# x in two token halves around the first modulation unit, context ahead of the last weights, index query and small projection at 356 columns

## The reference

```python
mod_x = (silu_c @ w_ada[i] + b_ada[i])[:, None, :]
sh1, sc1, g1, sh2, sc2, g2 = jnp.split(mod_x, N_MOD, axis=-1)
hx = modulate(rms_norm(x, norm1_g[i]), sh1, sc1)      # first block
hc = modulate(rms_norm(ctx, norm1_g[i]), csh1, csc1)  # ctx: 256 tokens
qx, kx, vx, ux = split_proj(hx @ w_in[i])
kvc = hc @ w_in[i][:, ATT_DIM:3 * ATT_DIM]
...
h = rmsnorm(x, norm_mix[layer])                       # second block
proj = h @ w_in[layer]
qa, ka, va, qb, kb, vb, qi, ki, wi, ga, gb = jnp.split(proj, IN_OFFSETS, axis=-1)
qi = rope(qi.reshape(B, T, IDX_HEADS, IDX_DIM), pos)
ki = rope(ki[:, :, None], pos)[:, :, 0]
```

## Time and profile before

| | us |
|---|---|
| median of 3 runs (729.28 to 729.64) | 729.4 |
| the profiled execution | 729.7 |
| its span | 727.9 |
| PE busy | 715.3 (98%) |
| PEld busy | 574.6 (79%) |
| DVE busy | 517.4 (71%) |
| ACT busy | 411.2 (56%) |
| POOL busy | 24.6 (3%) |

### The profile page before, as it was taken

One profiled execution on the slowest core, in us unless ns is written; L12 is line 12 of the kernel. 1 busy time (PEld: TensorE's weight loads), 2 busy tenths in 40 slices (PEclk: granted clock), 3 DMA queues, 4 the chain that ended last, 5 costly groups with the idle time before them and its releaser, 6 DMA issues.

```text
span 727.9 us, 9700 instructions
## 1 busy us (share of the span) xinstructions
PE 715.3 (98%) x3766; PEld 574.6 (79%) x3766; DVE 517.4 (71%) x911; ACT 411.2 (56%) x691; POOL 24.6 (3%) x43
## 2 busy tenths in 40 slices
PE   7999999999999999999999999999999999999996
PEld 6668885578888888888888777778888888888885
DVE  4689999898666866847898799765857455545544
ACT  4477658986754563556546676675455444344432
POOL 1030012001000000000110000000000000000000
PEclk9999999999999999999999999999999999999999
DMA  9995939617556576643548333453376566555511
GB/s 367 413 378 184 389 105 359 222 59 259 194 186 233 206 280 222 242 174 115 161 167 301 140 117 121 159 178 121 116 231 231 174 185 204 189 174 174 174 58 59
DMA packets 72990, 145.94 MB, mean 201 GB/s; under 512 B 4129, under 2 KB 27681, under 8 KB 71921
## 3 DMA queue, kind: packets, MB, share of 16 engines
q1 hardware_dynamic: 71136, 140.03, 55.0%
q0 software_dynamic: 1520, 5.03, 1.9%
q10 hardware_dynamic: 288, 0.27, 0.1%
HBM read 144.27 MB, written 1.05 MB: 200 GB/s over the span
## 4 chain that ended last, share of the span: by engine, by line
PE 87%; DVE 5%; ACT 2%; DMA 2%; issue 2%; SPq 0%; POOL 0%; POOLq 0%; DVEq 0%
PE bank L441 22%; PE bank L443 22%; PE bank L442 22%; PE bank L785 5%; PE bank L423 5%; PE bank L783 3%; DMA WX<-in_w_ada 2%; DVE WL L1573 2%; PE bank L460 1%; PE bank L917 1%; PE bank L939 1%; PE bank L623 1%; PE bank L782 1%; PE bank L514 1%; PE bank L481 1%
## 5 line engine op out<-in xcount | busy, mean ns | idle before, releaser
L1573 DVE TENSOR_TENSOR WL<-W,WH 128x1024 fp32r<-128x1024 f32 (+2 forms) x222 | 249.6, 1170 | 36.2 <-ACT WH L1070 36.1
L1070 ACT ACTIVATE WH<-W 128x1024 fp32r<-128x1024 f32 (+2 forms) x222 | 211.8, 1011 | 52.2 <-DMA W<-in_w_mlp 36.3
L441 PE MATMUL bank<-WH,AHL 128*128 128x512 f32 (+1 forms) x480 | 189.1, 394 | 0.8 <-DVE WL L1573 0.4
L443 PE MATMUL bank<-WH,AHL 128*128 128x512 f32 (+1 forms) x480 | 185.4, 386 | 0.0
L442 PE MATMUL bank<-WL,AHL 128*128 128x512 f32 (+1 forms) x480 | 185.2, 386 | 0.0
L441 PEld LDWEIGHTS bank<-WH,AHL 128*128 128x128 f32 x480 | 90.2, 188 | 22.8 <-issue 4.0
L443 PEld LDWEIGHTS bank<-WH,AHL 128*128 128x128 f32 x480 | 90.1, 188 | 18.6
L442 PEld LDWEIGHTS bank<-WL,AHL 128*128 128x128 f32 x480 | 90.3, 188 | 16.9
L441 PE MATMUL bank<-WH,HH 128*128 128x512 f32 (+1 forms) x218 | 84.9, 390 | 0.0
L443 PE MATMUL bank<-WH,HL 128*128 128x512 f32 (+1 forms) x218 | 84.5, 388 | 0.0
L442 PE MATMUL bank<-WL,HH 128*128 128x512 f32 (+1 forms) x218 | 84.4, 387 | 0.0
(11 more groups left out here) (287 smaller groups left out, 852.8 us busy)
## 6 DMA issues: line engine op xcount, KB each, us to landing
W<-in_w_mlp SPq DMA_DIRECT2D x32, 1024.0 KB, 5.4
W<-in_w_in SPq DMA_DIRECT2D x24, 1024.0 KB, 5.7
W<-in_w_gate SPq DMA_DIRECT2D x22, 512.0 KB, 4.2
W<-in_w_up SPq DMA_DIRECT2D x22, 512.0 KB, 5.2
W<-in_w_down SPq DMA_DIRECT2D x11, 1024.0 KB, 5.0
W<-in_w_ada SPq DMA_DIRECT2D x10, 1024.0 KB, 8.5
WX<-in_w_ada SPq DMA_DIRECT2D x10, 1024.0 KB, 10.4
W<-in_w_out SPq DMA_DIRECT2D x8, 1024.0 KB, 5.7
```

Of the source, the lines that this page charges most:

```text
L441: e.matmul(po, hs, wh[:, k, c0:c0 + cw], start=first and k == 0, stop=False)
L443: ins = e.matmul(po, ls, wh[:, k, c0:c0 + cw], start=False, stop=last and k == unit.nk - 1)
L1070: e.activation(m.WH[unit.slot][:, c], m.W32[unit.slot][:, c], ACT.Copy).then_inc(S["w_hi"], 1)
L1573: e.tensor_tensor(m.WL[unit.slot][:, c], m.W32[unit.slot][:, c], m.WH[unit.slot][:, c].bitcast(F32), ALU.subtract).then_inc(S["w_lo"], 1)
```

## The change

- **x by tokens.** `XT` and `xsq` are laid out as two halves of 128 tokens with all eight k. SP issues x half 0, modulation unit 0, x half 1, then the rest. ACT squares each half in two operations; the adds of DVE (`xpair`, `xfour`) are gone, and PE sums each half with eight matmuls of one column. Statistic, power and spread are done for each half by itself, and `modulate_x`, `high_x`, `low_x` of k = 0 too. On PE the order is now `mod_first(0)`, spread 0, turn 0, sums 1, `ab(0, 0)`, spread 1, `mod_first(1)`, turn 1, `ab(0, 1)`; from e8 = 1 on as before. Fewer idle matmuls (`keep_busy`).
- **Context.** `XC` is loaded ahead of the last `ab` unit. ACT: first square of the context, high part of the last `ab` unit, `high_x(7)`, high part of a `k` unit, second square, high part of the next. DVE: first statistic inside the step k = 7, first scaling, low part, second statistic, second scaling, low part.
- **356 columns.** The units `qi` hold the first 356 columns of the index query, the units `s` its last 156 columns with the 200 small ones. The list's order is qi, qi, s, s, qb, qb, and PE's order in `first2` qi, s, qb, with tile 1's transposes between the two halves of tile 0's `qb`. ACT copies one bank more for each tile. In ACT's second `between` the unit is split in two halves, one behind the second square of the first half of X and one behind the first square of the second half, not in one piece; the `hi(2)` behind it stays. The order of DVE's rope calls and ACT's copies follows the new counts.

```diff
@@ Mem
-        self.XT = M("XT", 0, [128, 8, 256])
-        self.xsq = M("xsq", 24, [128, 8, 256])
+        self.XT = M("XT", 0, [128, 2, 8, 128])
+        self.xsq = M("xsq", 40, [128, 2, 8, 128])
@@ weight_units
-    two("qi", "w_in_2", 2176, True, "qi_mm", (3, 4))
+    two("qi", "w_in_2", 2176, True, "qi_mm", (3, 4), 356)
+    for i in range(2):
+        add("s", "w_in_2", 4 * i, 4, [("w_in_2", 2532, 156), ("w_in_2", 2048, 128), ("w_in_2", 2688, 72)], True, ("s_mm", 3 + i))
     two("qb", "w_in_2", 1536, True, "p2_mm", (3, 4))
-    for i in range(2):
-        add("s", "w_in_2", 4 * i, 4, [("w_in_2", 2048, 128), ("w_in_2", 2688, 72)], True, ("s_mm", 3 + i))
@@ sync_program
-    for h in range(2):
-        e.dma_start(m.XT[:, 4 * h:4 * h + 4, :], d["xt"][h].rearrange("p (k t) -> p k t", k=4)).then_inc(S[f"l_x{h}"], 16)
-    for n in range(16):
+    x_half(0)
+    load(0)
+    x_half(1)
+    for n in range(1, 15):
         load(n)
     e.dma_start(m.XC[:, :, :], d["ctx"].rearrange("(t p) n -> p t n", p=128)).then_inc(S["l_xc"], 16)
-    for n in range(16, len(units)):
+    for n in range(15, len(units)):
@@ tensor_program
+    def x_sums(tb):
+
+        for k in range(8):
+            w.wait_ge(S["sq_sum" if k > 3 else "x_sq"], tb + 1)
+            ins = e.matmul(bank[5 + tb][:, 0:1], m.xsq[:, tb, k, :], m.ones[:, 0:1], start=k == 0, stop=k == 7)
+        ins.then_inc(S["sums"], 1)
+        frees(5 + tb, ("mean_sq", tb + 1))
...
+    keep_busy(7)
     x_sums(0)
+    keep_busy(2)
+    mod_first(0)
+    x_spread(0)
+    mod_turn(0, 4)
     x_sums(1)
+    ab(0, 0)
+    x_spread(1)
+    frees(7, ("setup", 5))
+    mod_first(1)
+    mod_turn(1, 6)
+    ab(0, 1)
+    for e8 in range(1, 8):
@@ first2
-        product(by["qi"], m.AH, m.AL, tb, 4 + tb, "qi_mm", n_ready(1, tb))
-        product(by["qb"], m.AH, m.AL, tb, tb, "p2_mm", n_ready(1, tb))
-        if tb == 0:
-            norm_turn(3, 1)
-        product(by["s"], m.AH, m.AL, tb, 2 + tb, "s_mm", n_ready(1, tb), 200)
+        product(by["qi"], m.AH, m.AL, tb, 4 + tb, "qi_mm", n_ready(1, tb), 356)
+        product(by["s"], m.AH, m.AL, tb, 2 + tb, "s_mm", n_ready(1, tb), 356)
+        product(by["qb"], m.AH, m.AL, tb, tb, "p2_mm", n_ready(1, tb), 512, None if tb else lambda: norm_turn(3, 1))
@@ scalar_program
-    hi()
     w.wait_ge(S["l_xc"], 16)
     square(2, m.XC[:, 0, :], m.XC2[:, 0, :])
+    hi()
     high_x(7)
+    hi()
     square(3, m.XC[:, 1, :], m.XC2[:, 1, :])
-    hi(2)
+    hi()
...
-    def between(tb, mid):
+    def between(tb):
         i = 8 + 4 * tb
+        halves = high_halves(tb)
         for n in range(2):
             for j in range(2):
                 w.wait_ge(S["btw"], 8 * tb + 3 * n + 2 + j)
                 square(i + 2 * n + j, m.X[:, tb, 512 * n:512 * n + 512], m.S1[:, tb, 512 * n:512 * n + 512])
-            hi(mid[n])
+                if n != j:
+                    next(halves, None)
...
     w.wait_ge(S["m2_mm"], 64)
     hi(2)
@@ vector_program
-            rows_out(k)
+    for k in range(1, 8):
+        rows_out(k)
         modulation(k)
         modulate_x(k)
+        if k == 7:
+            mean_square(2, (2,))
         lo()
         low_x(k)
-    mean_square(2, (2,))
+    hat(m.XC, m.XC2, 0, 2, "c_hat")
+    lo()
     mean_square(3, (3,))
-    lo()
-    hat(m.XC, m.XC2, 0, 2, "c_hat")
     hat(m.XC, m.XC2, 1, 3, "c_hat")
     lo()
```

More of the change, by code:

```diff
@@ L510, in ab @@
         ls = m.AL[:, e8, tb * 128:tb * 128 + 128]
-        w.wait_ge(S["mx_act"], e8 + 1)
+        w.wait_ge(S["mx_act"], e8 + 2 if e8 else tb + 1)
         for n in range(2):
@@ L521, in ab, with x_spread @@
                      stop=e8 == 7).then_inc(S["b_mm" if n else "a_mm"], 1)
[L523 to L533, removed]
-        w.wait_ge(S["l_id"], 16)
[L535 to L542, removed]
+    def x_sums(tb):
[4 more added lines that the diff above has]
+        frees(5 + tb, ("mean_sq", tb + 1))
+    def x_spread(tb):
+        w.wait_ge(S["l_id"], 16)
+        w.wait_ge(S["rstd"], tb + 1)
+        e.matmul(bank[7][:, tb * 128:tb * 128 + 128], m.stat[:, 40 + tb:41 + tb].to_broadcast([128, 128]), m.ident[:, :],
+                 start=True, stop=True).then_inc(S["sums"], 1)
+    keep_busy(7)
     x_sums(0)
-    keep_busy(3)
+    keep_busy(2)
+    mod_first(0)
+    x_spread(0)
+    mod_turn(0, 4)
     x_sums(1)
[L546 to L550, removed]
+    ab(0, 0)
[5 more added lines that the diff above has]
+    for e8 in range(1, 8):
         if e8 < 7:
@@ L887, in tensor_program @@
         product(by["ka"], m.AH, m.AL, tb, tb, "p2_mm", n_ready(1, tb))
[L888 removed]
+        frees(tb, ("p2_out", tb + 11))
         dots(4 * tb)
@@ L1086, in from_bank, with high_x @@
         copy(o, bank[b][:, cols], done, scale)
-    def high_x(k):
-        w.wait_ge(S["mx_dve"], k + 1)
-        e.activation(m.AH[:, k, :], m.hT[:, k, :], ACT.Identity, bias=m.mod1[:, k, 0, 0:1]).then_inc(S["mx_act"], 1)
+    def high_x(k, ts=slice(0, 256)):
+        w.wait_ge(S["mx_dve"], k + 2 if k else ts.stop // 128)
+        e.activation(m.AH[:, k, ts], m.hT[:, k, ts], ACT.Identity, bias=m.mod1[:, k, 0, 0:1]).then_inc(S["mx_act"], 1)
     def modulate_c(i, n):
@@ L1105, in two, with x_square @@
         return hT[:, 2 * i:2 * i + 2, :].rearrange("p a b -> p (a b)")
-    def half_of(t, h):
-        return t[:, 4 * h:4 * h + 4, :].rearrange("p a b -> p (a b)")
+    def x_square(tb):
+        w.wait_ge(S[f"l_x{tb}"], 16)
+        for h in range(2):
+            ks = slice(4 * h, 4 * h + 4)
+            e.activation(m.xsq[:, tb, ks, :], m.XT[:, tb, ks, :], ACT.Square,
+                         scale=1.0 / 32).then_inc(S["sq_sum" if h else "x_sq"], 1)
     e.dma_start(m.cs[:, :], d["cs"]).then_inc(S["l_cs"], 16)
@@ L1112, in scalar_program @@
     e.activation(m.cs[:, :], m.cs[:, :], ACT.Silu).then_inc(S["silu_c"], 1)
[L1113 to L1116, removed]
+    x_square(0)
+    x_square(1)
+    first = high_halves(1)
+    next(first)
+    high_x(0, slice(0, 128))
+    next(first)
+    next(first, None)
+    high_x(0, slice(128, 256))
+    for k in range(1, 7):
         hi()
         high_x(k)
-        if k == 1:
+        if k == 2:
             e.activation(m.stat[:, 92:93], m.stat[:, 94:95], ACT.Sigmoid)
-    hi()
     w.wait_ge(S["l_xc"], 16)
     square(2, m.XC[:, 0, :], m.XC2[:, 0, :])
+    hi()
     high_x(7)
+    hi()
     square(3, m.XC[:, 1, :], m.XC2[:, 1, :])
-    hi(2)
+    hi()
     for tb in range(2):
@@ L1663, in vector_program, with x_mean @@
     e.tensor_copy(m.csp[:, :, 0:2], m.cs[:, :].rearrange("p (k r) -> p k r", r=2)).then_inc(S["setup"], 1)
-    for h in range(2):
-        w.wait_ge(S["sq_sum"], h + 1)
-        tt(flat(m.xpair[h][:, :, :]), two(m.xsq, 2 * h), two(m.xsq, 2 * h + 1), ALU.add, "x_adds")
-        w.wait_ge(S["x_adds"], 2 * h + 1)
-        tt(m.xfour[h][:, :], m.xpair[h][:, 0, :], m.xpair[h][:, 1, :], ALU.add, "x_adds")
-    w.wait_ge(S["sums"], 1)
-    for tb in range(2):
-        e.tensor_scalar(col(24 + tb), bank[6 + tb][:, 0:1], EPS, None, ALU.add).then_inc(S["mean_sq"], 1)
-    rows_out(0)
-    for k in range(8):
-        if k:
-            rows_out(k)
+    def x_mean(tb):
+        w.wait_ge(S["sums"], (1, 3)[tb])
+        e.tensor_scalar(col(24 + tb), bank[5 + tb][:, 0:1], EPS, None, ALU.add).then_inc(S["mean_sq"], 1)
+    x_mean(0)
+    rows_out(0)
+    modulation(0)
+    modulate_x0(0)
+    first = low_halves(1)
+    next(first)
+    x_mean(1)
+    next(first)
+    next(first, None)
+    low_x(0, slice(0, 128))
+    modulate_x0(1)
+    e.tensor_copy(m.rB[:, :], bank[7][:, 0:256]).then_inc(S["setup"], 1)
+    low_x(0, slice(128, 256))
+    for k in range(1, 8):
+        rows_out(k)
         modulation(k)
         modulate_x(k)
+        if k == 7:
+            mean_square(2, (2,))
         lo()
         low_x(k)
-    mean_square(2, (2,))
+    hat(m.XC, m.XC2, 0, 2, "c_hat")
+    lo()
     mean_square(3, (3,))
-    lo()
-    hat(m.XC, m.XC2, 0, 2, "c_hat")
     hat(m.XC, m.XC2, 1, 3, "c_hat")
@@ L1826, in conv_centre @@
     def conv_centre():
-        w.wait_ge(S["sums"], 3)
+        w.wait_ge(S["sums"], 5)
         for c in range(4):
@@ L1849, in conv_scale @@
     def conv_scale():
-        w.wait_ge(S["sums"], 5)
+        w.wait_ge(S["sums"], 7)
         w.wait_ge(S["conv_act"], 1)
```

103 lines of the change are left out of this document (55 added, 48 removed).

## The result

The changed kernel took 736.5 us (733.42 to 739.07 in four executions), the kernel before beside it 729.5: a ratio of 1.0094, 95% interval 1.0067 to 1.0121. Slower, as forecast, but by 7 us instead of 2, and outside the range of 729.9 to 733.3. Its executions also differ among themselves far more than those of before (729.28 to 730.45), and that is the first clue: something in it is not fixed by the program.

The account below looks back on a forecast made before the run. PE was taken to bound the kernel, its chain running over PE for 87% of the span. Terms 2.0 + 0 + 0.1 = 2.1 us more gave 731.8 us profiled, 731.5 for the median, range 729.9 to 733.3.

Parts of the forecast that it names:

- part 2: New product order, first tile: PE waits for `qb`'s low halves, 2.6 us hole ahead of `qb`; +2.0 us taken.
- a rival at 0.15: Larger hole, about 733 us; a clock fall behind it would add 2.8 us to 12 matmuls; chance 0.15.
- part 3: Start, x in token halves: hidden under the fourth modulation unit's landing at 21.7 us; 0, up to +0.6 us.
- part 4: Context ahead of the last weights: second scaling ends at 49.9 us, PE's transposes 0.1 us later; +0.1, bounds -0.3 and +0.9.
- part 1: Widths 356 and 356 for 512 and 200: matmuls 0.162 us apart, 0.34 us less per tile.

Follow-up runs that it names:

- mid_fill: `mid_only` with eight matmul calls of 128 columns on ones between the small projection and `qb` of the first tile: 731.24 us (1.0028).
- mid_only: The kernel before with only the 356-column units and the new order of products; start and context as before: 732.75 us (1.0041).
- after_again: The changed kernel once more, unchanged, beside the kernel before: 736.16 us (1.0084); its profiled execution took 737.24 us.
- start_wide: The kernel before with only x halves, their shorter fill and the context's order, sums of x made 128 columns wide: 729.33 us against 729.33 (1.0004).
- ctx_only: The kernel before with only the context's load one unit earlier and its new order of squares, splits, means and scalings: 728.31 us (0.9987).
- no_hole: `mid_only` with ACT's first `qb` split ahead of its power wait and DVE's low halves ahead of two scalings: 729.27 us against 729.26 (0.9999).
- ctx_nohole: The kernel before with the edits of `ctx_only` and `no_hole` joined: 728.50 us (0.9986).

## Why the prediction was right and wrong

**The hole (part 2): right in place and size.** The forecast had PE waiting for DVE's low half, the scaling at 363.8 and the low half at 366.7; measured, less the 1.1 us by which the changed kernel was late there, 364.54 - 1.1 = 363.4 and 367.52 - 1.1 = 366.4. The wait inside the small projection is 1.1 us, forecast 1.2, and the one ahead of `qb` 2.3, forecast 2.6 (there the text counted to 366.8, 0.1 us past its own 366.7). The 731.24 of `mid_fill` and the 731.18 of the one short execution of `mid_only` are this term alone: +1.8 to +2.0 for a forecast of +2.0. The transposes lay inside `qb`, and behind 385 us no new wait appeared.

**The clock behind the hole: the step that failed first.** The text held the fall for a rival at 0.15, because PE had 1.00 in the first 9 us though busy only 5.86 of them. That row could not bear this: `after_again` has 1.00 in that column while its matmuls run at half speed, so the column says nothing of a clock that has not risen yet. The timeline of PE in the kernel before shows it too, in its first fill, 0.20 us a record where the later one of six takes 0.14:

```profile
2.76 4.40 PE L500 MATMUL bank<-ones 128*128 128x128 f32 x22 [2.76 <-POOL ones L360]
...
10.92 0.83 PE L500 MATMUL bank<-ones 128*128 128x128 f32 x6
```

The rival priced 12 matmuls at +2.8 us; measured are 1.5 to 1.7, since only some 7 to 9 of them are hit, by 0.20 us each. The Trainium skill (TensorE: Matmul & The Clock Gate, What's actually happening) lets an idle array go back to half clock. `mid_only` and `mid_fill` agree with it; in the profiled execution of `after_again` the same hole passed without a fall. Which executions fall is not settled.

**The start (part 3): the step that was mis-sized worst.** The count of PE's instructions was right, 16 records of some 0.115 us a half. What failed is the price of one record. It came from the earlier trace rows, at full clock, and the sum took the clock for given. With 7 calls of fill ahead of them, the clock had in the longer executions not risen when the 16 one-column matmuls came: 0.213 us a record, and double length for all until as late as 22 us. In others it rose and fell again behind the second 16, as in the first profile. The forecast of 0, up to +0.6, comes near only in the mended form, where the fourth modulation begins at 22.08 (21.76 before); there PE's own chain and not the landing is last, 0.9 us later than the 21.2 worked out, and `start_wide` stands 1.0 us behind `ctx_only`. As changed the start costs 5.7 us. A rival in which one-column matmuls leave the clock low was missing altogether, although the diff removed 4 of the 11 calls ahead of the first sums whose only work is to keep PE busy. That edit was never costed by itself; with wide sums it costs nothing (`start_wide`).

**The context (part 4): wrong sign.** The forecast of +0.1, with -0.3 as its lower end, took 1.2 us for each scaling, half of the pair at 47.42. In `ctx_only` each takes 0.75, and the first went where DVE had waited. So the low part starts at 44.5, forecast 45.5, and the second scaling ends at 48.3, forecast 49.9; POOL's 0.66 us behind the late statistic came as written. The term was -1.0, with the lower bound set too high. DVE's timeline in the kernel before had the shorter price for the same shape:

```profile
366.21 0.75 DVE L1585 TENSOR_SCALAR X<-X,stat 128x1024 f32<-128x1024 f32 x1 [0.27 <-ACT S L1078]
```

**The widths (part 1): right in size, nothing in the sum.** Between 356.28 and the end of the index query the matmuls stand 0.163 us apart, forecast 0.162. The gain of 0.7 us in two tiles is not seen in `no_hole` (an interval of some 0.6 us either way), nor in `ctx_nohole` against `ctx_only`. The profile of `no_hole` shows half of it: the second tile takes from 370.23 to 383.53, 13.3 us instead of 13.7, but the first, with waits of some tenths in its small projection, 15.7 (354.56 to 370.23) instead of 15.6. Why the median shows not even that half is open.

**The sum.** 2.0 + 0 + 0.1 = 2.1 was forecast. The parts alone give +5.7 for the start and +3.3 for the rest, 9.0, and together 6.7 (736.16 against 729.42). These are medians over executions that lie on different steps, so they need not add. In the profiled execution of `after_again` the long start comes without a fall behind the hole, and 737.24 is near 735.1 + 1.8. But the two longest executions of the first measurement, 738.83 and 739.07, have a mean granted clock of 0.996, as the executions of `mid_only` with the fall, and lie near 735.1 + 3.3: in them both losses seem to come in full. They weren't profiled, so that isn't shown.

## What to carry to other kernels

Cost matmuls of few columns at both clocks: here PE was busy nearly all the time and its clock still stayed at 1.2 GHz or fell to it, and widening the one-column matmuls to 128 columns cost 0.1 us and gave back 5.7. When a diff takes away instructions that only keep an engine busy, give that edit a line of its own in the sum, and look at the lengths of known shapes, not only at the clock column. When units of work change places in a list, follow each unit through the other engines' fixed order: here one split of ACT moved ahead of a wait, and low halves of DVE ahead of two scalings, were worth 3.5 us.

## What the runs showed of the hardware

- One-column and 128-column matmuls of the sums take nearly the same time at full clock, 1.84 and 1.95 us for 16. In the runs here the clock stayed at 1.2 GHz until 14 to 22 us with the former, or fell from 2.4 behind them with PE busy for 3.87 of 4.00 us; with the latter the one profile shows neither, and none of eleven executions took over 730.5 us.
- A DVE scaling of 128x1024 took 1.2 us in the kernel before at 47.42 (two in 2.35), beside DMA issues and memsets of POOL, and 0.75 in `ctx_only`. But the second one in `ctx_only` also ran beside a DMA issue of POOL (47.46 to 48.41), so what makes it long, the memsets or something else, isn't shown. POOL's memset was longer in the kernel before too, beside a scaling, than in `ctx_only`, beside a low part of DVE:

```profile
48.13 0.63 POOL L371 MEMSET hp<- 128x68 f32 x1
```

```profile
49.54 0.18 POOL L371 MEMSET hp<- 128x68 f32 x1
```

The Trainium skill (GPSIMD Engine Reference, Specifications) says that the two share SBUF interfaces and can contend there. The memset's two lengths agree with that; no run here varied POOL's work alone.
